# Neighbourhood scores of two heads issued together on the row halves, and both maxima ahead of the normalisations

## What is computed

```python
s_loc = jnp.einsum('bwhd,biwjhd->bhwij', q_r, k_win).reshape(B, H, GRID_W, n_loc)
s_ctx = jnp.einsum('bwhd,bchd->bhwc', q_r, k_ctx)
s = jnp.concatenate([s_loc.astype(jnp.float32) * scale + bias,
                     s_ctx.astype(jnp.float32) * scale], axis=-1)
p = jax.nn.softmax(s, axis=-1).astype(v.dtype)
```

## Time and profile before

| | us |
|---|---|
| median of 3 runs | 1900.77 |
| lowest and highest | 1898.17, 1901.21 |
| the profiled execution | 1899.83 |
| its span, first to last instruction | 1898.0 |
| PE busy | 1665.0 (88%) |
| DVE busy | 593.5 (31%) |
| ACT busy | 322.5 (17%) |
| neighbourhood half of attention, layer 0 | about 290 to 342 |
| neighbourhood half of attention, layer 1 | about 1272 to 1303 |

### The profile page before, as it was taken

The page is one execution under the profiler, slowest core; times in us unless marked ns, Lnnn a source line. Parts: engine busy times, 40 slices in busy tenths (PEclk is TensorE's granted clock), DMA queues, the critical chain, the costliest instruction groups (busy, mean ns, idle before and its releaser), DMA issues.

```text
span 1898.0 us, 21646 instructions
## 1 busy us (share of the span) xinstructions
PE 1665.0 (88%) x9099; PEld 873.8 (46%) x9099; DVE 593.5 (31%) x1108; ACT 322.5 (17%) x794; POOL 95.5 (5%) x174
## 2 busy tenths in 40 slices
PE   5999999999999998979889899999998666676666
PEld 2656454444477332424222367777885323232222
DVE  3745334464664112112121423444413111010101
ACT  3223333200023010100001322343011000000001
POOL 5001100000021000000000000200000000000000
PEclk9999999999999999999999999999999877687888
DMA  9615005244485999999999631316957999999996
GB/s 357 216 59 150 1 1 200 88 156 147 142 343 208 356 413 421 421 421 421 421 422 421 266 123 43 88 45 244 332 229 325 421 421 421 421 421 421 420 421 289
DMA packets 132044, 528.33 MB, mean 278 GB/s; under 512 B 9966, under 2 KB 74644, under 8 KB 76396
## 3 DMA queue, kind: packets, MB, share of 16 engines
q1 hardware_dynamic: 129260, 523.64, 69.8%
q0 software_dynamic: 2688, 3.32, 1.0%
HBM read 525.84 MB, written 1.07 MB: 278 GB/s over the span
## 4 chain that ended last, share of the span: by engine, by line
PE 61%; DMA 34%; DVE 3%; ACT 1%; issue 1%; SPq 0%; DVEq 0%; ACTq 0%
DMA ring<-in_w_e_dram 33%; PE ps L840 14%; PE ps L1134 10%; PE ps L1344 8%; PE ps L1179 4%; PE ps L1143 4%; PE ps L1370 4%; PE ps L1094 3%; PE ps L1056 2%; PE ps L752 2%; PE ps L952 2%; PE ps L1277 1%; DMA ring<-in_w_mod_dram 1%; PE ps L1078 1%; PE ps L1305 1%; PE ps L938 1%
## 5 line engine op out<-in xcount | busy, mean ns | idle before, releaser
L1344 PE MATMUL ps<-ring,arena 128*32 128x256 f32 (+1 forms) x2856 | 376.8, 504 | 110.7 <-DMA ring<-in_w_e_dram 107.9
L1344 PEld LDWEIGHTS ps<-ring,arena 128*32 128x32 f32 (+1 forms) x2856 | 122.7, 128 | 344.5 <-DMA ring<-in_w_e_dram 173.7
L1370 PE MATMUL ps<-ring,arena 128*32 128x256 f32 (+1 forms) x1496 | 208.5, 539 | 67.1 <-DMA ring<-in_w_e_dram 65.6
L1134 PE MATMUL ps<-arena,ring 128*128 128x512 f32 (+1 forms) x576 | 191.8, 486 | 0.0
L840 PE MATMUL ps<-arena,ring 128*128 128x512 f32 (+1 forms) x480 | 176.5, 523 | 0.0
L1370 PEld LDWEIGHTS ps<-ring,arena 128*32 128x32 f32 (+1 forms) x1496 | 67.3, 135 | 205.0 <-issue 101.1
L2225 DVE COPY arena<-ps 32x512 f32<-32x512 f32 (+1 forms) x124 | 68.6, 553 | 277.8 <-PE ps L1370 276.5
L1134 PEld LDWEIGHTS ps<-arena,ring 128*128 128x128 f32 x576 | 109.1, 190 | 76.5 <-issue 68.3
L1715 ACT ACTIVATE arena<-ps 128x512 f32<-128x512 f32 (+1 forms) x32 | 15.7, 491 | 728.9 <-PE ps L1344 728.9
L2218 DVE TENSOR_TENSOR arena<-arena,ps 128x512 f32<-128x512 f32 (+1 forms) x32 | 17.8, 555 | 374.5 <-PE ps L1344 374.5
L840 PEld LDWEIGHTS ps<-arena,ring 128*128 128x128 f32 x480 | 90.0, 191 | 80.5 <-issue 76.7
(11 more groups left out here) (234 smaller groups left out, 1399.0 us busy)
## 6 DMA issues: line engine op xcount, KB each, us to landing
ring<-in_w_e_dram SPq DMA_DIRECT2D x364, 1024.0 KB, 17.8
ring<-in_w_in_dram SPq DMA_DIRECT2D x44, 1024.0 KB, 9.1
ring<-in_w_mod_dram SPq DMA_DIRECT2D x40, 1024.0 KB, 9.6
arena<-in_w_e_dram SPq DMA_DIRECT2D x17, 1024.0 KB, 7.6
ring<-in_w_out_dram SPq DMA_DIRECT2D x8, 1024.0 KB, 11.2
arena<-in_w_mod_dram SPq DMA_DIRECT2D x8, 1024.0 KB, 14.7
arena<-in_w_br_ml_dram SPq DMA_DIRECT2D x8, 512.0 KB, 5.7
ring<-maxima SPq DMA_DIRECT2D x2, 1024.0 KB, 4.8
```

Of the source, the lines that this page charges most:

```text
L1134: mm = pe.matmul(ps[:, u % 3, tq], wg[:, k, cols], hT[:, k, tq], start=k == 0, stop=k == KD - 1)
L1344: mm = pe.matmul(ps[M * j:M * j + M, m, 0:NW], XSTs[l][e // GROUP % 2][:, kk, e % GROUP, 0:M], w[:, k, j * NW:(j + 1) * NW], start=kk == 0 ...
L1370: mm = pe.matmul(ps[M * j:M * j + M, 3, 0:NW], lhs, w[:, k, j * NW:(j + 1) * NW], start=kk == 0, stop=kk == KD - 1)
```

## The change

Three edits. In PE's loop the na half (steps from nu // 2 on) issues no score in odd steps and two, of units i and i + 1, in even ones. The scores of such a pair both wait for the exponentials of all units before the pair, so the first waits for unit i - 1 where it waited for unit i - 2. In DVE's loop the even steps of that half make the maxima of both units, and the odd steps none, so that the order is normalise(i - 1), row_max(i), row_max(i + 1), head(i - 4), normalise(i). Gate products, transposes, values, ACT's and SP's programs stay as they are, and so does the MLA half.

```diff
--- before.py
+++ after.py
@@ -1047,7 +1047,7 @@
                     kind, h, t = L.units[i]
                     nkey = T if t >= 2 else CTX
                     if i >= 2:
-                        pe.wait_ge(sem("attn_exp"), before("attn_exp", l) + i - 1)
+                        pe.wait_ge(sem("attn_exp"), before("attn_exp", l) + (i - i % 2 if kind == "na" else i - 1))
                     p0 = 64 * (h % 2)
                     if kind == "mla":
                         a, b = qT[0:QK, h, t * P:(t + 1) * P], kT[0:QK, h, 0:nkey]
@@ -1108,7 +1108,11 @@
                         pe.wait_ge(sem("proj_taken"), last_projection)
                         pe.wait_ge(sem("roped"), before("roped", l) + 1)
                     if i < nu:
-                        score(i)
+                        if i < nu // 2:
+                            score(i)
+                        elif i % 2 == 0:
+                            score(i)
+                            score(i + 1)
                         gate_products(max(4, 6 * KD * i // nu), max(4, 6 * KD * (i + 1) // nu))
                     if 1 <= i <= nu:
                         turn(i - 1)
@@ -2036,8 +2040,11 @@
                 for i in range(nu + 3):
                     if 1 <= i <= nu:
                         normalise(i - 1)
-                    if i < nu:
+                    if i < nu // 2:
                         row_max(i)
+                    elif i < nu and i % 2 == 0:
+                        row_max(i)
+                        row_max(i + 1)
                     if i >= 4 and i % 2 == 0:
                         head(i - 4)
```

## The result

The changed kernel takes 1888.57 us (median of 5 runs, 1886.14 to 1889.94) against 1900.77 (1898.17 to 1901.25). The ratio is 0.9941, with an interval from 0.9929 to 0.9953: 8.9 to 13.5 us less. Forecast was 1890.8.

The account below looks back on a forecast made before the run. PE was taken to bound the neighbourhood half of attention. Savings of 6.4 us in layer 0 and 3.6 in layer 1, together 10.0, took 1900.77 us to a forecast of 1890.8, range 1887.8 to 1897.0.

Parts of the forecast that it names:

- PE bounds the stage: Neighbourhood half of attention: PE sets its length, 52.85 us busy of 54.00 in layer 0, 27.81 of 29.00 in layer 1.
- One block for two scores, 1.25 us saved: PE, neighbourhood pairs: both row halves overlap fully, one 1.05 us block, saving 1.25 with 512 keys, 0.82 with 256.
- The wait ahead of the first head's transposes, 4.53 us after the score block's start: Layer 1's 512-key pairs: VectorE's chain ends at 4.53 us, PE arrives at 4.18 and waits 0.35.
- the 0.06 for the weight load: First head's transposes: 0.06 us added to the 4.47 us chain for a weight load a waiting PE can't do ahead.
- some eight waits of 0.3 to 0.6: Sign in the trace: PE waits for the scaling ahead of the first head's transposes, eight times 0.3 to 0.6 us.
- pair to pair 6.1: Sign in the trace: layer 1's 512-key pairs follow each other every 6.1 us, against 6.99 before.
- The new wait is covered by 0.9 us: First score of a pair: the exponential just before it ends some 0.9 us ahead of need, so the wait costs nothing.
- Everything passes through: Stages behind the neighbourhood halves, DMA-bound experts too, all move forward, so the whole 10.0 us reaches the end.
- Steps: Rival, paired scores: strict program order makes a 512-key block 1.48 us; 8.7 us saved, time 1892.1; chance 0.14.
- Halves queue: Rival, paired scores: the row halves don't overlap, only the trips are saved, 4.7 us, time 1896.1; chance 0.13.
- Given back: Rival, layer 0's merge or experts: their loads are the limit, 6.4 us lost, 3.6 kept, time 1897.2; chance 0.08.
- Slower by the clock: Rival, neighbourhood stage: PE's pauses drop the clock to 1.2 GHz; 1913.8 us with half of layer 0's stage; chance 0.05.

Follow-up runs that it names:

- e3: The changed kernel with the odd head's score reading the even head's partitions, so both scores use the same row half; ratio 0.9979 to the kernel before.
- e7: The kernel before with only the new wait added: even neighbourhood scores wait for the exponential of the unit just before; ratio 0.9999 to the kernel before.
- e1: The changed kernel with VectorE's old order of maxima and normalisations restored, PE still issuing paired scores; ratio 0.9946 to the kernel before.
- e5: The changed kernel with layer 1 put back to the old order, so the change acts in layer 0 alone; ratio 0.9956 to the kernel before.
- e6: The changed kernel with layer 0 put back to the old order, so the change acts in layer 1 alone; ratio 0.9971 to the kernel before.
- e4: The changed kernel with VectorE's head copy moved behind the first head's normalisation; ratio 0.9936 to the kernel before.

## Why the prediction was right, and where its sizes were off

*PE bounds the stage.* Right: only what moved PE's instructions or made it wait moved the stage.

*One block for two scores, 1.25 us saved.* Right. Block 1.06 instead of the forecast 1.05; with 256 keys 0.81 per pair, forecast 0.82 (in layer 0 296.65 less 291.56 is 5.09, was 5.90). Full overlap, taken from column strips, holds for row halves too, and e3 gives the price of its absence. No row of before had shown two row halves side by side, so this step was a guess from the nearest rows that came out.

*The wait ahead of the first head's transposes, 4.53 us after the score block's start.* The mechanism is right, and this is the mis-sized term: it measured 4.23 (1274.60 to 1278.83). I had added isolated durations with a gap of 0.03 to 0.04 behind each. Queued VectorE instructions that wait for nothing start ahead of their predecessor's recorded end: the second bias add starts at 1276.84 while the reduction's record runs to 1276.92; add to add is 1.08, where I had 1.15, add to head copy 1.06, where I had 1.18, and head copy to reciprocal 0.20, where I had 0.26 to 0.28. The earlier trace rows had it to be seen: the head copy starts at 1281.33, while the reduction of 1280.72 runs 0.69, to 1281.41. Nor was the 0.06 for the weight load part of the arrival; it lies behind it (transposes to values 0.58 instead of 0.53). So a 512-key pair saved 1.16 in layer 1 (forecast 0.90), and in layer 0 0.91 behind 256 keys (forecast 0.67; 6.32 went to 5.41) and 1.14 behind 512 (forecast 0.88). Eight pairs by 0.24 to 0.26 are the 2 us by which the stages' 11.96 exceed the forecast 10.0. Of the signs named ahead, "some eight waits of 0.3 to 0.6" and "pair to pair 6.1" did not come: the trace has two waits of 0.27 and six of about 0.05, and 5.83.

*The new wait is covered by 0.9 us.* Right in its effect: no score of the changed kernel waited for an exponential, and e7 shows the wait at zero with the old order. The cover was larger. The second head's exponential is through at 1278.96, 4.36 after the score block's start (the 4.34 of the prediction; its 5.16, with two copies in between, did not come), and the next score starts at 1280.44: 1.48 us. All of this cover is the work of the maxima's order, as with the old one (e1) nothing of it is left.

*Everything passes through.* Right, by e5 and e6. In single executions it can't be read as simply as the prediction had it (merges 6.4 and 10.0 us earlier): they start 6.07 and 13.78 us earlier, since stretches outside the two halves differ too (last section). In layer 1 SP's wait for the end of attention was halved, from 10.5 to 5.0 us, so a further saving of more than about 5 us there might meet the DMA; no run tests that.

*Rivals.* Steps: out, by the two first passes that start together and the block of 1.06 instead of 1.48. Halves queue: out for the change, and by e3 its price was right to 0.1 us (4.67 against 4.7). Given back: out. Slower by the clock: the neighbourhood halves were granted 1.00 with the pauses in, as this table of stages of the changed kernel (columns as in the earlier trace rows) shows:

```profile
288.00:338.00 50.00, 48.16 (x274) 25.09 (x273) 24.57 (x71) 24.51 (x61) 0.00 (x0) 1.00 0.55 192
1262.00:1290.00 28.00, 26.58 (x199) 19.20 (x200) 15.31 (x39) 14.56 (x34) 0.00 (x0) 1.00 0.91 325
```

I had taken the chance of the clock from nothing better than the 0.80 of a stage whose pauses are another kind, and the pauses came out at 0.27 us and less, so longer ones in this stage were not tested.

## What to carry to other kernels

If two matmuls use 64 rows each, in different halves of the array, and write to different banks, issue them back to back: here the second one was free, and one trip to the half array and back (0.39 us) was saved for each pair. An order like that takes a partner on the reading engine: work out the chain on VectorE from start to start of queued instructions, not from durations with gaps, and check which of the two orders is left waiting. When the work on an engine is the bound, measure its stage from fixed points in the trace; here that repeated to 0.02 us where the time of whole runs spread over several.

## What I had not expected

The spans of the two profiled executions differ by 13.7 us (1898.0 against 1884.3), the stages by 11.96. The largest other difference, 2.2 us, lies in a stretch that the change doesn't touch, the start of layer 1 (17.71 us from the first matmul of L875 to the first projection before, 15.56 after). Before, the stage by stage view, and the chain of waits for one group in it:

```profile
1080.00:1088.00 8.00, 5.87 (x48) 5.30 (x47) 7.58 (x14) 7.27 (x21) 1.85 (x9) 1.00 0.00 0
1088.00:1092.00 4.00, 2.23 (x16) 2.19 (x16) 4.00 (x14) 2.04 (x6) 0.25 (x2) 0.90 0.01 2
1092.00:1096.00 4.00, 2.40 (x14) 0.60 (x16) 0.34 (x2) 1.51 (x4) 0.00 (x0) 0.50 0.00 0
```

```profile
1093.86 3.64 PE ps L896 x16
```

and after:

```profile
1073.00:1081.00 8.00, 6.07 (x48) 5.56 (x48) 7.46 (x13) 7.23 (x21) 1.65 (x8) 1.00 0.00 0
1081.00:1085.00 4.00, 2.03 (x17) 1.86 (x16) 4.00 (x14) 2.30 (x7) 0.46 (x3) 1.00 0.01 2
1085.00:1089.00 4.00, 2.40 (x19) 0.85 (x19) 0.60 (x2) 1.83 (x5) 0.00 (x0) 1.00 0.00 0
```

```profile
1086.68 1.92 PE ps L896 x16
```

The same 16 passes took 3.64 us at a granted clock of 0.50, that is 1.2 GHz, and 1.92 at 1.00; the rest of the 2.2 us is the block of L875 ahead of them, 2.49 instead of 2.05. In both executions PE had been busy for only 6 of 8 us and then 2 of 4 before it; in one the clock fell and in the other it did not. The group took 3.64 us in e4 and 3.21 in e1 as well, whose pair orders are near the change's, and 1.92 in the other seven runs. In e7, whose order is that of before, the clock fell too, but in the block of L875, which took 3.58 us, and it was back at 1.00 for the group. So it fell at this place in four of the eleven executions shown here, with old and new orders among them: it isn't tied to the change. What decides it in one execution or another stays open. Smaller differences (layer 0's half starts 1.3 us later in the changed kernel, and 0.7 us are saved between its merge and layer 1) make up most of the rest and were not looked into.
